# Large weights stored as contiguous 2 MB pieces, 16 KB to a partition

## The reference

```
for i in range(2):
    shift, scale, gate (twice) = silu(cond) @ w_ada[i] + b_ada[i]
    h = x * (1 + scale) + shift
    o = hyena(h) if i == 0 else attention(h)      # hy_w_in, hy_w_out / na_w_qkv, na_w_out
    x = layer_norm(alpha * x + gate * o)
    t = x * (1 + scale2) + shift2
    pick the best of 4 groups, then the best 2 of its 4 experts; c = their weights
    for e in range(16):
        a, b = split(t @ w_up[e])                  # 1024 x 1024
        y += c[:, e] * ((silu(a) * b) @ w_down[e]) # 512 x 1024
    x = layer_norm(alpha * x + gate2 * y)
```

## Time and profile before

| | us |
|---|---|
| median of 3 runs | 1044.7 |
| lowest, highest | 1043.2, 1046.48 |
| the profiled execution, its time | 1044.42 |
| the profiled execution, its span | 1042.6 |
| PE busy, of the span | 977.5 (94%) |
| DVE busy | 714.0 (68%) |
| moved by DMA | 318.29 MB, 305 GB/s in the mean |

### The profile page before, as it was taken

One profiled execution on the slowest core, in us unless ns is written; L12 is line 12 of the kernel. 1 busy time (PEld: TensorE's weight loads), 2 busy tenths in 40 slices (PEclk: granted clock), 3 DMA queues, 4 the chain that ended last, 5 costly groups with the idle time before them and its releaser, 6 DMA issues.

```text
span 1042.6 us, 28278 instructions
## 1 busy us (share of the span) xinstructions
PE 977.5 (94%) x11348; PEld 578.3 (55%) x11348; DVE 714.0 (68%) x1905; ACT 189.4 (18%) x443; POOL 195.1 (19%) x304
## 2 busy tenths in 40 slices
PE   8999999999699999999899999999979999999883
PEld 2555556565456656666455554575545566666441
DVE  6458884956766666666769995474676676766457
ACT  4342223012210000000140013462231000000003
POOL 1400000620132222222100001254013222222111
PEclk9999999999999999999989999999989999999896
DMA  9964666950999999999996588832097999999991
GB/s 330 400 257 163 230 243 223 391 182 23 355 340 405 405 406 405 406 405 405 394 401 235 212 326 323 285 102 73 6 354 287 371 405 405 404 405 405 406 372 66
DMA packets 102207, 318.29 MB, mean 305 GB/s; under 512 B 8402, under 2 KB 12690, under 8 KB 101747
## 3 DMA queue, kind: packets, MB, share of 16 engines
q1 hardware_dynamic: 92228, 298.87, 74.5%
q0 software_dynamic: 5776, 17.30, 4.9%
q10 hardware_dynamic: 4128, 1.05, 0.4%
HBM read 311.44 MB, written 5.77 MB: 304 GB/s over the span
## 4 chain that ended last, share of the span: by engine, by line
PE 76%; DMA 7%; DVE 6%; SPq 6%; issue 2%; POOL 1%; ACT 1%; DVEq 0%
PE bank L824 74%; SPq L539 5%; DMA ring<-in_moe_w_down 4%; DMA ring<-in_w_ada 3%; POOL P L792 1%; PE bank L1332 1%; DVE P L2232 1%; PE bank L871 1%; DVE st L2169 0%; PE bank L1039 0%; DVE x L2283 0%; PE bank L883 0%; DVE sc L1979 0%; DVE x L2284 0%; PE bank L863 0%
## 5 line engine op out<-in xcount | busy, mean ns | idle before, releaser
L824 PE MATMUL bank<-ring,xgT 128*32 128x256 f32 x4224 | 246.1, 384 | 8.0 <-DMA ring<-in_moe_w_up 4.9
L824 PE MATMUL bank<-hT,ring 128*128 128x384 f32 x640 | 207.2, 486 | 0.0
L824 PEld LDWEIGHTS bank<-ring,xgT 128*32 128x32 f32 x4224 | 148.7, 111 | 97.7 <-issue 22.0
L824 PEld LDWEIGHTS bank<-hT,ring 128*128 128x128 f32 x640 | 121.4, 190 | 85.6 <-issue 1.8
L1734 DVE CUSTOM_DVE_ANT_0 ring<-ring,ring 128x1024 f32<-128x1024 f32 x112 | 137.0, 1224 | 3.7 <-DMA ring<-in_k_ada 0.3
L824 PE MATMUL bank<-ring,heT 128*32 128x256 f32 x2112 | 129.4, 383 | 5.0 <-DMA ring<-in_moe_w_down 4.6
L2119 DVE TENSOR_TENSOR he<-sa,bank 128x64 f32<-128x64 f32 x132 | 26.6, 201 | 131.9 <-ACT sa L1569 131.9
L1569 ACT ACTIVATE sa<-bank 128x128 f32<-128x128 f32 x66 | 18.3, 277 | 424.1 <-PE bank L824 424.1
L824 PEld LDWEIGHTS bank<-ring,heT 128*32 128x32 f32 x2112 | 62.7, 109 | 53.6 <-DVE heT L2121 14.0
L824 PE MATMUL bank<-yt,ohT 32*128 32x256 bf16 x2448 | 81.4, 271 | 2.5 <-DVE yt L2149 1.9
L758 POOL DMA_INDIRECT group_row<-token_rows,rows_now x68 | 73.9, 1087 | 17.6 <-issue 17.3
(11 more groups left out here) (298 smaller groups left out, 1188.8 us busy)
## 6 DMA issues: line engine op xcount, KB each, us to landing
ring<-in_moe_w_up SPq DMA_DIRECT2D x64, 2048.0 KB, 23.6
ring<-in_moe_w_down SPq DMA_DIRECT2D x32, 2048.0 KB, 21.0
ring<-in_k_ada SPq DMA_DIRECT2D x14, 2048.0 KB, 11.0
ring<-in_w_ada SPq DMA_DIRECT2D x10, 2048.0 KB, 14.9
ring<-in_na_w_qkv SPq DMA_DIRECT2D x6, 2048.0 KB, 17.4
ring<-in_hy_w_in SPq DMA_DIRECT2D x5, 2048.0 KB, 11.7
ring<-in_hy_w_out SPq DMA_DIRECT2D x2, 2048.0 KB, 10.6
ring<-in_na_w_out SPq DMA_DIRECT2D x2, 2048.0 KB, 12.8
```

The source lines that it names most:

```text
L824: return nc.tensor.matmul(out, lhsT, rhs, start=first, stop=last)
```

## The change

The host writes the large weights once more, in another order: `in_pieces(w, k)` takes k blocks of 128 rows and stores, for each partition p, its k rows one behind the other. A piece is then a contiguous array of 128 x 4096 fp32 in HBM, with 16 KB for each partition. `laid_out` does it for the pieces of `w_ada` that PE uses (`k_seg`, in the order of `COND_SEG`), for `hy_w_in`, `na_w_qkv`, the two output weights, and the experts' up and down weights; `k_ada0` and `k_ada1` go through `in_pieces` too. The original arrays are no longer passed. In the kernel only the source and the shape of each transfer change: `ring[slot][:, :]` from a contiguous piece, in place of k rows. What lies in SBUF after it is the same, byte for byte, and PE's and DVE's code is untouched. The first piece of `hy_w_in` stays in two halves, now of 8 KB for each partition. The number of transfers, their sizes, their order, their waits, and the order of the instructions on every engine are the same.

```diff
@@ -199,8 +199,27 @@
     for i, n in enumerate(("hy_f_b1", "hy_f_b2", "hy_f_freq")):
         mlp[:, MLP_COL + i] = np.tile(A[n][0], 2)
     rows = {f"k_ada{l}": np.ascontiguousarray(A["w_ada"][l][:, 512 * DOTS[l][0]:512 * DOTS[l][-1] + 512].T) for l in range(DEPTH)}
+    rows = {n: in_pieces(r, 4) for n, r in rows.items()}
     conds = np.concatenate([A["c_ctx"].reshape(-1), A["c"].reshape(-1)])
     return {"k_first": np.ascontiguousarray(first, np.float32), "k_mlp": mlp, "k_cond": np.ascontiguousarray(conds, np.float32), **rows}
+
+
+def in_pieces(w, k):
+
+    n = w.shape[-1]
+    return np.ascontiguousarray(w.reshape(*w.shape[:-2], -1, k, 128, n).swapaxes(-3, -2)).reshape(*w.shape[:-2], -1, 128, k * n)
+
+
+def laid_out(A):
+
+    def by_columns(w):
+
+        return np.stack([in_pieces(w[:, at_:at_ + 512], 8)[0] for at_ in range(0, w.shape[1], 512)])
+
+    return {"k_seg": np.stack([in_pieces(A["w_ada"][l][:, 512 * n:512 * n + 512], 8)[0] for _, l, n in COND_SEG]),
+            "k_in": by_columns(A["hy_w_in"][0]), "k_qkv": by_columns(A["na_w_qkv"][0]),
+            "k_out": np.stack([by_columns(A[n][0]) for n in ("hy_w_out", "na_w_out")]),
+            "k_up": in_pieces(A["moe_w_up"], 4), "k_down": in_pieces(A["moe_w_down"], 4)[:, :, 0]}
 
 
 def neighbour_bias(rpb):
@@ -517,10 +536,9 @@
                             return
                 sp.wait_ge(group_ready, last_group(j) + 1)
 
-            def load(i, src, k):
+            def load(i, src):
                 wait_slot_free(i)
-                sp.dma_start(w_view(i, k, 4096 // k), src.rearrange("(k p) n -> p k n", p=128)
-                             ).then_inc(w_loaded[W_SLOT[i]], 16)
+                sp.dma_start(ring[W_SLOT[i]][:, :], src).then_inc(w_loaded[W_SLOT[i]], 16)
 
             def load_biases(which):
 
@@ -532,12 +550,11 @@
                     sp.dma_start(bm[:, m % 3, :, 0:SAMPLE], A["na_bias"][m]).then_inc(bias_in[m % 3], 16)
 
             def experts(l):
-                up, down = A["moe_w_up"][l], A["moe_w_down"][l]
+                up, down = A["k_up"][l], A["k_down"][l]
                 first = W_AT[f"moe{l}"]
 
                 def piece(i, src):
-                    sp.dma_start(w_view(i, 4, 1024), src.rearrange("o (k p) n -> p (o k) n", p=128)
-                                 ).then_inc(w_loaded[W_SLOT[i]], 16)
+                    sp.dma_start(ring[W_SLOT[i]][:, :], src.rearrange("o p n -> p (o n)")).then_inc(w_loaded[W_SLOT[i]], 16)
 
                 S = moe_sems[l]
 
@@ -575,7 +592,7 @@
                         sp.wait_ge(S["gathered"], 1)
                     elif slot == RING + 4:
                         sp.wait_ge(S["x_added"], 1)
-                    piece(first + i, up[who, c * 512:(c + 1) * 512, :] if c < 2 else down[who, :, :])
+                    piece(first + i, up[who, c, :, :] if c < 2 else down[who, :, :])
                 for e in range(EXPERTS - 4, EXPERTS):
                     if e not in groups_through[l]:
                         count_groups(l, e)
@@ -588,7 +605,7 @@
 
             def cond(k):
                 seg, l, n = COND_SEG[k]
-                load(W_AT[seg], A["w_ada"][l][:, n * 512:(n + 1) * 512], 8)
+                load(W_AT[seg], A["k_seg"][k])
 
             def load_named(name):
 
@@ -599,16 +616,15 @@
                     i = W_AT[name]
                     wait_slot_free(i)
                     for b, landed in enumerate((in0_half, w_loaded[W_SLOT[i]])):
-                        sp.dma_start(w_view(i, 8, 512)[:, 4 * b:4 * b + 4, :],
-                                     A["hy_w_in"][0][512 * b:512 * b + 512, 0:512].rearrange("(k p) n -> p k n", p=128)).then_inc(landed, 16)
+                        half = slice(2048 * b, 2048 * b + 2048)
+                        sp.dma_start(ring[W_SLOT[i]][:, half], A["k_in"][0, :, half]).then_inc(landed, 16)
                 elif kind == "in":
-                    load(W_AT[name], A["hy_w_in"][0][:, int(n) * 512:(int(n) + 1) * 512], 8)
+                    load(W_AT[name], A["k_in"][int(n)])
                 elif kind == "qkv":
-                    load(W_AT[name], A["na_w_qkv"][0][:, int(n) * 512:(int(n) + 1) * 512], 8)
+                    load(W_AT[name], A["k_qkv"][int(n)])
                 elif kind.startswith("dot"):
                     l = int(kind[3:])
-                    r = 512 * (int(n) - DOTS[l][0])
-                    load(W_AT[name], A[f"k_ada{l}"][r:r + 512, :], 4)
+                    load(W_AT[name], A[f"k_ada{l}"][int(n) - DOTS[l][0]])
                 else:
                     i = W_AT[name]
                     wait_slot_free(i)
@@ -633,14 +649,14 @@
                     sp.wait_ge(group_ready, G_AT["decay3"] + 1)
                     sp.dma_start(skip[0:1, :], bass.AP(A["hy_d"].tensor, A["hy_d"].offset, [[D, 1], [1, D]])).then_inc(skip_in, 16)
             for s in range(OUT_W):
-                load(W_AT["out0"] + s, A["hy_w_out"][0][:, s * 512:(s + 1) * 512], 8)
+                load(W_AT["out0"] + s, A["k_out"][0, s])
             experts(0)
             for name in LOAD_ORDER[LOAD_ORDER.index("cond7"):LOAD_ORDER.index("out1")]:
                 if name == "qkv_0":
                     rows_after_experts(0)
                 load_named(name)
             for s in range(OUT_W):
-                load(W_AT["out1"] + s, A["na_w_out"][0][:, s * 512:(s + 1) * 512], 8)
+                load(W_AT["out1"] + s, A["k_out"][1, s])
             experts(1)
             rows_after_experts(1)
 
@@ -2304,7 +2320,8 @@
     tables, feat, cols = shape_constants()
     arrays.update(tables)
     arrays.update(side_by_side(arrays, feat, cols))
-    for n in ("b_ada", "c", "c_ctx", "hy_b_in", "hy_conv_w", "hy_conv_b", "hy_f_w1", "hy_f_w2", "hy_f_b1", "hy_f_b2", "hy_f_freq"):
+    arrays.update(laid_out(arrays))
+    for n in ("moe_w_up", "moe_w_down", "w_ada", "hy_w_in", "na_w_qkv", "hy_w_out", "na_w_out", "b_ada", "c", "c_ctx", "hy_b_in", "hy_conv_w", "hy_conv_b", "hy_f_w1", "hy_f_w2", "hy_f_b1", "hy_f_b2", "hy_f_freq"):
         arrays.pop(n)
     aps = {n: nc.dram_tensor(f"in_{n}", a.shape, mybir.dt.from_np(a.dtype), kind="ExternalInput").ap()
            for n, a in arrays.items()}
```

## The result

| | median of the runs | profiled execution | its span |
|---|---|---|---|
| before, beside it | 1044.68 us (6 runs, 1042.89 to 1047.07) | 1044.4 us | 1042.6 us |
| changed | 1039.15 us (6 runs, 1036.43 to 1041.38) | 1039.6 us | 1037.7 us |

The ratio is 0.9944, with a 95% interval of 0.9929 to 0.9958: faster by 4.4 to 7.4 us, where 12.8 were forecast. A repetition is among the experiments.

What follows compares the result with a forecast made beforehand. PE was taken as the bound, with transfers binding only at the ends of the two layers' experts. 1044.42 - 6.3 (layer 1) - 6.5 (layer 0) = 1031.6 us; forecast 1029 to 1036, 8 in 10 range 1025 to 1041.

Steps and rivals of the forecast that it cites:

- The packet's cost: All weight transfers: with 16 KB runs a piece takes 0.17 us less than with 4 KB rows, 0.40 less than with 2 KB.
- my line: Packet time against size, drawn through 2 and 4 KB packets: 414 GB/s at 8 KB, 419 at 16 KB.
- The stretch 860 to 960: Sign in layer 1's expert stream: the rate goes from 405 to 417 GB/s or more.
- The end of layer 1: Last of 37 expert pieces lands 6.3 us earlier, between 4 and 9; PE still waits for it by about 2 us.
- it holds, closely; if it failed, the lost part would be at most 1 us: Layer 1's expert stream: the weight queue does not run dry although pieces are issued only as PE frees slots.
- the place that I had named: Tightest point of layer 1's queue, the piece issued at 887.98: 3.5 us of queue left, 2.6 taken by the change.
- The end of layer 0: After layer 0's experts: PE's 3.87 us wait on `w_ada` goes, the clock stays full; 6.5 us gained.
- the clock falls anyway: Rival's condition at the end of layer 0: the clock still drops, leaving 3.5 us there; whole rival's chance 0.10.
- The chain behind it: After the `w_ada` wait: PE and ACT work independent of transfers lets x tiles turn at about 521.7, 5.9 us earlier.
- What costs nothing: Start pieces (0.40 us each, hidden), the 14 DVE pieces and the instructions: no effect on the time.
- the first rival: Gathers under the expert stream land after 15.2 us and become the bound: about 1150 us; chance 0.05.
- only one place pays: Clock falls at the end of layer 0 and the queue runs dry in layer 1: 3.5 + 3.5, or 1037 us; chance 0.10.

Runs made afterwards that it cites:

- half pieces: Changed kernel, but from the twelfth piece of each layer on expert pieces bring only half of each partition's run (results wrong): 1026.97 us, ratio 0.9838 to before.
- both of these: Changed kernel with 4 KB rows for the first four experts of each layer, plus matmuls whose result nobody reads: 1037.34 us, ratio 0.9921 to before.
- 8 KB runs: Changed kernel, but each partition's 16 KB comes as two runs of 8 KB, for all large weights: 1040.38 us, ratio 0.9956 to before.
- All but experts: Kernel before, with all large weights except the experts' in 16 KB runs: 1043.52 us, ratio 0.9983 to before.
- experts alone: Kernel before, with only the experts' up and down weights in 16 KB runs: 1039.56 us, ratio 0.9935 to before.

## Why the prediction was wrong

**The packet's cost: right, a little too small.** The forecast had 0.17 us less for a piece of 4 KB rows. The start of the kernel runs at 423 GB/s and the 30 us before 860 at 424, above the 419 of my line; 423 instead of 405 makes 0.22 us a piece. From the first landing of the stretch to the last, 36 pieces later, it is 196.2 us before (817.8 to 1014.0) and 191.3 after (816.1 to 1007.4): 4.9 us, or 7.0 with the 2.1 that the thin places lost, which is 0.19 a piece. The stretch 860 to 960, where I asked for 417, gives 413, because both thin places of layer 1 lie in it. The page of the Trainium skill ("DMA: Bandwidth & Descriptors", section "Bandwidth") has 425 GB/s for a transfer of 16 MB; 423 agrees with it.

**The end of layer 1: right in kind, 6.3 was 4.5 to 5, and the queue did not hold.** PE still waits for the last piece by over 2 us, as said. But "it holds, closely; if it failed, the lost part would be at most 1 us" failed: the stream fell to 328 GB/s around the issue at 887.17, the place that I had named, and to 342 around that at 919.61, which I had not looked at, and lost some 2 us. In each of the nine profiles with 16 KB runs in most of layer 1's experts (half pieces apart) at least one stretch of 5 us at these places reads 324 to 364 GB/s. From the first issue to the last landing it is 205.50 us before (808.51 to 1014.01) and 199.94 after (807.45 to 1007.39): 5.56 us less. These are counted from the first issue, and in the changed kernel that issue comes 17.6 us after the first up of layer 1 instead of 16.6, after the second group that waits for its gather. What is left is 222.2 and 222.9 against 217.6 and 217.8 in the table. The larger saving of the packet hid part of what the thin places cost; that 6.3 came out as near as it did is in part luck.

**The end of layer 0: this step failed.** The forecast took the wait of 3.87 us on `w_ada` as a property of the kernel and its removal as the gain, and added what a full clock would give: 6.5 us. Two things were wrong in it. The wait is the difference of two times of which one varies by 3.7 us from execution to execution; the profile of before that I read was one with PE early, and in its second profile the wait is 0.70. And the clock does fall: its lower level is granted in parts of the stretch from 516 to 537 us in every profile, with no idle time above 1.3 us ahead of it in the changed kernel, while I expected full clock below 1.6 us of idle time. From first up to first up, which holds the whole of it, before has 495.7 and 495.0, and the seven profiles with 16 or 8 KB runs in most of layer 0's experts (changed, twice, to "both of these") 492.5 to 496.5, 494.6 in the middle. So it is 0.8 us in the middle; 3.2 when both profiles compared have no pause, and that alone is near the 3.5 that I gave for "the clock falls anyway".

Cut at PE's first step on `w_ada` the two parts show the exchange. From the first up to this step it is 218.7 and 222.4 us in the two profiles of before, and 219.0 to 222.7 in the seven, 221.6 in the middle. From this step to the first up of layer 1 it is 277.0 and 272.6 in before, and 272.1 to 274.9 in the seven, 273.4 in the middle. So the removal of the long wait is worth 3.6 us where PE is early, and nothing where PE is late. The chain behind it was nearly as forecast: with no wait and a full clock on the two steps, the values start 10.85 us after the first of them (8 KB runs: 518.93 to 529.78), where the forecast had about 10.

**What costs nothing: the first gathers cost up to 1 us.** They are on PE's path after the start of the experts. That DVE already waited 0.8 us for one of them in before was a row that I did not look for, since PE had no wait there. It is 0.3 to 1.0 us more to the second group of layer 0 where its pieces have 16 KB packets. I had looked at the gathers in the steady part alone, where 7.7 us instead of 6.0 are indeed hidden: the first rival rightly had little chance, but a mild form of it was sure.

The first up of layer 0 is late too, at 297.3 to 297.9 instead of 296.2 in five of these seven profiles. That is not the gathers, the first of which POOL issues at 295.86: the lateness is there 35 us after the start. PE, before and changed:

```profile
34.59 1.02 PE L824 MATMUL bank<-cond_sum,arow 128*128 128x2 f32 x8 [0.81 <-ACT arow L1398]
```

```profile
35.56 1.02 PE L840 MATMUL bank<-cond_sum,arow 128*128 128x2 f32 x8 [0.81 <-ACT arow L1414]
```

In the fourteen profiles this step starts between 34.2 and 35.9 us, and the first up 261.6 to 262.6 us after it. "All but experts" has 16 KB runs at the start and 34.34; "experts alone" has 2 KB rows there and 35.22. So the layout does not decide it; what does was not tried.

**The sum again.** With the middle values of these seven against the mean of the two profiles of before: first up +1.2, to the first up of layer 1 -0.8, to the last awaited down -4.9 (217.7 against 222.6), tail 0: -4.5 us, against a measured -5.5 (4.4 to 7.4 by its interval); without the first up, which is chance of the profiles, -5.7. So layer 1 brought nearly all of it. Of the rivals "only one place pays" (1037) was nearest, and both of its conditions came true: the clock fell, and the queue ran thin in layer 1. What it did not have is the larger part of what was missing: PE comes late to the end of layer 0 in most profiles, so that there is little wait to remove.

## What to carry to other kernels

A wait read from one profile is one difference of two arrivals: before counting its removal as a gain, take a second profile and see which of the two moves, since a wait that absorbs chance delays gives back less than it shows. Where transfers set the end of a stretch, count per transfer what a longer run saves, check it by the last landing, and look for every place where the queue is short: a faster stream reaches it sooner and then waits for slots. A bigger packet delays small transfers on other queues by a bounded amount (1.3 to 1.7 us here), which costs only where such a transfer is on the path, mostly right after the first one is issued.

## What the hardware showed that I had not expected

With 2 KB rows the stream moved at 388 GB/s, with 4 KB at 405, with 8 KB runs at 418 (830 to 860 us of that kernel) and with 16 KB at 424: the last doubling brings 1.4%. The clock can fall after an idle time of only 0.97 us, as in both profiles of the changed kernel (at about 516.5 and 519.5 us), where up to 5.34 us instead of 3.64 go into the same 32 records; in the other nine profiles with this idle time it did not fall there. And PE stops for 0.5 and 0.8 to 1.4 us near 470 us in nine of fourteen profiles, between or within groups of matmuls, with nothing in PE's records that releases it.
